# A two-layer attention and mixture-of-experts kernel: the pair's rows are added to DRAM tables too, projections and softmax steps change places, and the layer loop is written out

## What is computed

```python
parts  = split(x @ w_in)                        # 2956 columns: q, k, v of three groups, index q/k/w, latents
mixed  = concat([fox(...), dsa(...), mla(...), chunk_band(...)])   # four groups of 4 heads, softmax over 256 keys
x      = layer_norm(ALPHA * x + mixed @ w_out)
scores = sigmoid(x @ w_router)                  # 64 experts, 8 of them for each token, gates normed
routed = sum_e gate[e] * ((silu(h[:, :256]) * h[:, 256:]) @ w_down[e]),  h = x @ w_gu[e]
shared = the same block without a gate
x      = layer_norm(ALPHA * x + routed + shared)
```

## Time and profile before

| | |
|---|---|
| median of 3 runs | 1805.72 us (1804.13 to 1807.51) |
| the profiled execution | 1801.29 us, of which the span is 1799.5 us |
| busy: TensorE, VectorE, ScalarE, GpSimd | 1664.7, 952.0, 765.8, 283.5 us |
| DMA | 529.71 MB, mean 294 GB/s |
| granted TensorE clock, mean | 0.973 |

### The profile page before, as it was taken

The page is one execution under the profiler, slowest core; times in us unless marked ns, Lnnn a source line. Parts: engine busy times, 40 slices in busy tenths (PEclk is TensorE's granted clock), DMA queues, the critical chain, the costliest instruction groups (busy, mean ns, idle before and its releaser), DMA issues.

```text
span 1799.5 us, 29297 instructions
## 1 busy us (share of the span) xinstructions
PE 1664.7 (93%) x10062; PEld 1260.4 (70%) x10062; DVE 952.0 (53%) x1445; ACT 765.8 (43%) x1020; POOL 283.5 (16%) x200
## 2 busy tenths in 40 slices
PE   6798899999999999999879989999999999999996
PEld 5697767766776677666668877666776667777763
DVE  1746455555555555555457455555555555555555
ACT  3464434343434443444246633444444444434342
POOL 6471000001000001000135700000010000000010
PEclk8899899999999999999989989999999999999998
DMA  9331599999999999999953327999999999999993
GB/s 312 95 118 59 208 335 350 345 346 350 341 350 353 356 352 352 353 341 336 338 182 115 118 71 287 345 349 342 356 355 351 346 351 354 354 341 349 347 356 113
DMA packets 141739, 529.71 MB, mean 294 GB/s; under 512 B 12236, under 2 KB 51576, under 8 KB 108408
## 3 DMA queue, kind: packets, MB, share of 16 engines
q1 hardware_dynamic: 122288, 467.77, 69.1%
q0 software_dynamic: 15440, 56.11, 11.2%
q10 hardware_dynamic: 3960, 5.17, 0.9%
HBM read 507.24 MB, written 21.77 MB: 294 GB/s over the span
## 4 chain that ended last, share of the span: by engine, by line
PE 64%; DMA 15%; DVE 7%; issue 5%; ACT 5%; DVEq 2%; SPq 1%; ACTq 0%; PEldq 0%
DMA raw<-in_w_exp_gu_dram 11%; PE ps L1083 11%; PE ps L1057 10%; PE ps L949 7%; PE ps L950 7%; PE ps L951 7%; PE ps L733 6%; PE ps L986 4%; PE ps L972 4%; ACT w_hi L1405 3%; DMA raw<-in_w_exp_down_dram 3%; DVE o_lo L1791 2%; PE ps L1124 2%; PE ps L979 2%; PE ps L865 1%
## 5 line engine op out<-in xcount | busy, mean ns | idle before, releaser
L1763 DVE TENSOR_TENSOR raw_r<-raw,w_hi 128x2048 fp32r<-128x2048 f32 x192 | 440.0, 2293 | 447.6 <-ACT w_hi L1405 447.5
L1405 ACT CAST w_hi<-raw 128x2048 fp32r<-128x2048 f32 x192 | 365.8, 1906 | 311.2 <-DMA raw<-in_w_exp_down_dram 203.9
L949 PE MATMUL ps<-x_hi,w_hi 128*128 128x256 f32 x1088 | 311.4, 286 | 1.8 <-DVE x_lo L1689 1.8
L950 PE MATMUL ps<-x_lo,w_hi 128*128 128x256 f32 x1088 | 306.9, 282 | 0.0
L951 PE MATMUL ps<-x_hi,raw_r 128*128 128x256 f32 x1088 | 306.3, 282 | 0.0
L1083 PE MATMUL ps<-raw,xc 128*64 128x512 f32 x1024 | 233.8, 598 | 0.0
L949 PEld LDWEIGHTS ps<-x_hi,w_hi 128*128 128x128 f32 x1088 | 206.6, 190 | 31.4 <-issue 30.1
L950 PEld LDWEIGHTS ps<-x_lo,w_hi 128*128 128x128 f32 x1088 | 207.9, 191 | 1.5
L951 PEld LDWEIGHTS ps<-x_hi,raw_r 128*128 128x128 f32 x1088 | 206.7, 190 | 0.0
L682 POOL DMA_INDIRECT xg_b<-x_by_token,token_b x32 | 31.3, 979 | 830.9 <-DVE token_c L1742 830.9
L1083 PEld LDWEIGHTS ps<-raw,xc 128*64 128x64 f32 x1024 | 67.8, 136 | 119.4 <-issue 115.0
(11 more groups left out here) (324 smaller groups left out, 2916.6 us busy)
## 6 DMA issues: line engine op xcount, KB each, us to landing
raw<-in_w_exp_gu_dram SPq DMA_DIRECT2D x256, 1024.0 KB, 8.0
raw<-in_w_exp_down_dram SPq DMA_DIRECT2D x128, 1024.0 KB, 7.7
raw<-in_w_in_dram SPq DMA_DIRECT2D x22, 1024.0 KB, 5.8
raw<-in_w_out_dram SPq DMA_DIRECT2D x8, 1024.0 KB, 5.2
row_b<-gates_by_rank SPq DMA_DIRECT2D x30, 256.0 KB, 5.8
row_c<-gates_by_rank SPq DMA_DIRECT2D x60, 128.0 KB, 5.3
raw<-in_w_sh_gu_dram SPq DMA_DIRECT2D x4, 1024.0 KB, 5.1
row_a<-gates_by_rank SPq DMA_DIRECT2D x32, 128.0 KB, 10.8
```

What stands on the lines that cost most here:

```text
L949: nc.tensor.matmul(o, h, x_hi[:, c, :], start=(first and i == 0), stop=False, skip_group_check=True)
L950: nc.tensor.matmul(o, h, x_lo[:, c, :], start=False, stop=False, skip_group_check=True)
L1405: nc.scalar.copy(w_hi[CAST[j] % 3][:], raw[:, j % RING, 0:UNIT_F]).then_inc(hi_done, 1)
L1763: nc.vector.tensor_tensor(raw_r[:, s, 0:UNIT_F], raw[:, s, 0:UNIT_F], w_hi[CAST[j] % 3][:], ALU.subtract)\
```

## The change

- **Pair's rows.** In steps 0 to 14 ACT copies the pair's output to a plain tile `o_c`, and POOL adds it with a second accumulating indirect DMA to the tables. There are two tables now (`added_rows` has `2 * TABLE` rows): class C1 goes to the first, C2 to the second. `o_lo` and the eight matmuls of `scatter` are left only in the last step, and `place_b`, `place_c` are built only there. POOL waits for the landing of the first accumulation, then issues the second and waits for that too. ACT and DVE wait for `o_c_free`.
- **Order of a step.** TensorE does `dense_down(0)`, C1D/C2D, `gathered_t(xg_b)`, `dense_down(1)`, `gathered_t(xg_c)`. SP loads the slots in the new order of use.
- **Last step.** C1D/C2D, scatter B, `dense_down(0)`, scatter C tile 0, then tile 1 in halves. Two more 512 KB loads bring the second table; DVE adds them.
- **Attention stage.** 13 jobs: `ik` comes out of unit 1's rows and is transposed, `f` out of unit 3's rows (260 wide). A projection is put before the transposes of the latents; the bias tables and the rounds of `mark_top` move behind the latents and in between the softmax steps. The first projection of a layer starts on `x_hi` alone.
- **Layer norms.** Tile 1 is taken in halves, each with a wait of its own. `shared_lo(0)` goes ahead of the last `mixed_low`, piece 1 goes to POOL. The shared expert's silu is issued after its gate half.
- **Clearing.** The tables are cleared (four 512 KB stores, before two) behind POOL's low parts instead of at the head of the layer.
- `with Fori(0, DEPTH)` becomes `for layer in range(DEPTH)` in all five streams.

```diff
@@ sync
-            with sp.Fori(0, DEPTH) as layer:
+            for layer in range(DEPTH):
-                        sp.wait_ge(unit_used, done(layer, unit_used, slot(k) - RING + 1))
+                        sp.wait_ge(unit_used, done(layer, unit_used, LAST_USES.index(slot(k)) - RING + 1))
-                    for j in range(RING):
+                    for j in LAST_USES:
@@ gpsimd
-            with pool.Fori(0, DEPTH) as layer:
-                for t in range(NT):
-                    pool.dma_start(added_rows[t * P:(t + 1) * P, :].rearrange("p (c n) -> p c n", n=P),
-                                   zeros[:].bitcast(F32).unsqueeze(1).to_broadcast([P, KC, P])).then_inc(sums_cleared, 16)
+            for layer in range(DEPTH):
...
+                for row in (0, P, TABLE, TABLE + P):
+                    pool.dma_start(added_rows[row:row + P, :].rearrange("p (c n) -> p c n", n=P),
+                                   zeros[:].bitcast(F32).unsqueeze(1).to_broadcast([P, KC, P])).then_inc(sums_cleared, 16)
+                pool.wait_ge(hi_done, done(layer, hi_done, 2))
+                pool.tensor_tensor(raw_r[:, slot(NPRE + 1), 0:UNIT_F], raw[:, slot(NPRE + 1), 0:UNIT_F], w_hi[1][:], ALU.subtract)\
+                    .then_inc(shared_lo1_done, 1)
...
                     pool.wait_ge(o_b_added, done(layer, o_b_added, it * 16 + 16))
                     pool.sem_inc(o_b_free, 1)
+                    pool.wait_ge(c_out_hi_sb, done(layer, c_out_hi_sb, it * 2 + 2))
+                    pool.sem_inc(pool_turn, 1)
+                    pool.indirect_dma_start(added_rows, bass.IndirectOffsetOnAxis(ap=token_out_c[:, 0:1], axis=0), o_c[:], None,
+                                            compute_op=ALU.add).then_inc(o_c_added, 16)
+                    pool.wait_ge(o_c_added, done(layer, o_c_added, it * 16 + 16))
+                    pool.sem_inc(o_c_free, 1)
@@ tensor: attention stage
-                columns(job(1)[0:IDM, 0:SEQ], layer, 1, 0, IDM, True).then_inc(job_ps, 1)
-                project_rows(2, 1)
-                pe.wait_ge(job_sb, done(layer, job_sb, 2))
+                project_rows(1, 1)
+                o = job(2)
+                rows(o, layer, 2, (0,))
+                pe.wait_ge(ik_rows_sb, done(layer, ik_rows_sb, 1))
+                for t in range(NT):
+                    last = nc.tensor.transpose(ps[:, 4, t * P:(t + 1) * P], ik_rows[:, t].rearrange("p r n -> p (r n)"), ident[:])
+                last.then_inc(ik_ps, 1)
+                rows(o, layer, 2, (1,)).then_inc(job_ps, 1)
+                pe.wait_ge(ik_sb, done(layer, ik_sb, 1))
                 index_dots(1)
-                project_rows(3, 2)
-                project_rows(4, 3)
-                columns(job(5)[0:NH, 0:SEQ], layer, 3, GW, NH, False).then_inc(job_ps, 1)
+                tile_rows(job(3), layer, 3, 0).then_inc(job_ps, 1)
+                tile_rows(job(4), layer, 3, 1).then_inc(job_ps, 1)
+
+                project_t(5, 4)
@@ tensor: tail of a step
-                    for t in range(NT):
-                        last = dense_down(t, *weights(AD))
-                    last.then_inc(unit_used, 1)
...
+                    if not final:
+                        dense_down(0, *weights(AD))
...
+                    if final:
+                        pe.wait_ge(place_b_ready, done(layer, place_b_ready, it + 1))
+                        pe.wait_ge(b_out_sb, done(layer, b_out_sb, 2))
+                        for t in range(NT):
+                            last = scatter(place_b, t)
+                        last.then_inc(b_added, 1)
+                        dense_down(0, *weights(AD))
+                        pe.wait_ge(place_c_ready, done(layer, place_c_ready, it + 1))
+                        pe.wait_ge(c_out_sb, done(layer, c_out_sb, 2))
+                        scatter(place_c, 0).then_inc(tile0_done, 1)
+                        for half in range(2):
+                            last = dense_down(1, *weights(AD), (half,))
+                            if half == 1:
+                                last.then_inc(unit_used, 1)
+                            scatter(place_c, 1, (half,)).then_inc(moe_done, 1)
+                    else:
                         pe.wait_ge(o_b_ready, done(layer, o_b_ready, it + 1))
                         pe.wait_ge(xg_b_loaded, done(layer, xg_b_loaded, it * 16 + 32))
                         gathered_t(xg_b, 0, xb_ps)
-                    pe.wait_ge(place_c_ready, done(layer, place_c_ready, it + 1))
-                    pe.wait_ge(c_out_sb, done(layer, c_out_sb, it * 2 + 2))
-                    for t in range(NT):
-                        last = scatter(place_c, t)
...
+                        dense_down(1, *weights(AD)).then_inc(unit_used, 1)
+                        pe.wait_ge(c_out_hi_sb, done(layer, c_out_hi_sb, it * 2 + 2))
                         pe.wait_ge(xb_lo_sb, done(layer, xb_lo_sb, it * 2 + 4))
@@ scalar
                     act.wait_ge(b_half_ps, done(layer, b_half_ps, it + 1))
+                    act.wait_ge(o_c_free, done(layer, o_c_free, it))
...
-                    nc.scalar.copy(o_hi[:, 0:512], ps[:, 2, :]).then_inc(c_out_hi_sb, 1)
+                    o = o_hi if final else o_c
+                    nc.scalar.copy(o[:, 0:512], ps[:, 2, :]).then_inc(c_out_hi_sb, 1)
@@ vector
+                        dve.wait_ge(o_c_free, done(layer, o_c_free, it))
+                        out_row(token_out_c, 1, table_col[:, 0:1])
...
-                    out_lo(c_out_hi_sb, c_out_sb, it, 2)
-                    if not final:
                         gathered_lo(it + 1, 0)
                         low(it + 1, A0)
```

More of the change, by code:

```diff
@@ L736, in columns @@
             def columns(o, layer, k, c0, n, first):
+                if k == 0 and first:
+                    wh, wl = high_part(k), in_slot(k, width(k), raw_r)
+                    for c in range(KC):
+                        if c % 4 == 0:
+                            pe.wait_ge(w_lo_ready, done(layer, w_lo_ready, c // 4 + 1))
+                        pe.wait_ge(xt_hi_sb, done(layer, xt_hi_sb, c // 2 + 1))
+                        nc.tensor.matmul(o, wh[:, c, c0:c0 + n], x_hi[:, c, :], start=(c == 0), stop=False)
+                        nc.tensor.matmul(o, wl[:, c, c0:c0 + n], x_hi[:, c, :], start=False, stop=False)
+                    for c in range(KC):
+                        pe.wait_ge(xt_sb, done(layer, xt_sb, c // 2 + 1))
+                        last = nc.tensor.matmul(o, wh[:, c, c0:c0 + n], x_lo[:, c, :], start=False, stop=(c == KC - 1))
+                    return last
                 return three(o, layer, k, slice(0, SEQ), c0, n, True, first)
@@ L980, in gathered_t, with scatter @@
                     last.then_inc(signal, 1)
-                def scatter(place, t):
-                    for half in range(2):
+                def scatter(place, t, halves=range(2)):
+                    for half in halves:
                         for part in (o_hi, o_lo):
@@ L997, in _ @@
                 last.then_inc(router_ps, 1)
-                for b in range(2 * NT):
-                    nc.tensor.matmul(ps[:, 4 + b, :], zeros[:], x_hi[:, 0:2, :], start=True, stop=False, skip_group_check=True)
                 shared_gate_up(1)
@@ L1031, in _ @@
                 nc.tensor.matmul(ps[0:NE, 2, :], perm[:], both, start=True, stop=True).then_inc(ranked_ps, 1)
+                for b in range(2 * NT):
+                    nc.tensor.matmul(ps[:, 4 + b, :], zeros[:], x_hi[:, 0:2, :], start=True, stop=False, skip_group_check=True)
                 pe.wait_ge(a_ready, done(layer, a_ready, 1))
-                pe.wait_ge(split_done, done(layer, split_done, SH))
+                pe.wait_ge(split_done, done(layer, split_done, SH - 1))
                 for t in range(NT):
@@ L1158, in _ @@
             act.dma_start(t5_dram, t5_row[:]).then_inc(t5_stored, 16)
-            with act.Fori(0, DEPTH) as layer:
+            for layer in range(DEPTH):
                 def split_pre(k, halves=range(2)):
@@ L1380, in _ @@
                 last.then_inc(mask_t_sb, 1)
+                act.wait_ge(shared_gate_ps, done(layer, shared_gate_ps, 1))
+                silu_dense(0)
                 act.wait_ge(gates_t_ps, done(layer, gates_t_ps, 1))
@@ L1500, in _ @@
                 dve.sem_inc(s, START[s])
-            with dve.Fori(0, DEPTH) as layer:
+            for layer in range(DEPTH):
                 for b in range(4):
```

350 lines of the change are left out of this document (195 added, 155 removed).

## The result

The kernel after takes 1713.86 us (median of four runs, 1708.98 to 1719.39) against 1806.62 beside it: ratio 0.9477, 95% interval 0.9428 to 0.9527. It is faster, and by twice what was forecast: 93 us by the medians, 84.8 by the two profiled executions (spans 1799.5 and 1714.7), where the prediction said 42 (1763 us, range 1735 to 1792).

What follows compares the result with a forecast made beforehand. TensorE (93% busy) and, in the mixture stages, the DMA queue were both taken as nearly full. Terms of -6, -9.3, +5, -10.2, -8.7, -2.2, -1, -11, -2 and +4 gave -42 us: 1763 us, range 1735 to 1792.

Steps and rivals of the forecast that it cites:

- Mixture step, DMA: Ordinary steps: 2.7 us idle, taken up by a second accumulation of 2.7; -0.2 us a step, -6 over 30 steps.
- the prediction's best ends: Low end of the forecast DMA work of a mixture step: 41.6 us, against 42.4 expected and 43.0 at worst.
- rival 1: Mixture steps: mixed traffic already at its 348 GB/s ceiling, step 44.0 us, +45 in place of -6, total 1814; chance 0.08.
- rival 2: Mixture steps: queue has room, holes take the whole accumulation; a step loses 1.4 us at 373 GB/s, total 1727; chance 0.13.
- Mixture step, TensorE: End of a step: eight matmuls and the o_lo wait go, 3.5 us on TensorE, at best 2.0 usable.
- Last steps: Last step of each layer: norm starts earlier, -9.3 us in all; against it +5 for loading more table.
- Narrow jobs, latents, moved top-k: Attention stage: narrow projections -10.2 us; latents -8.7, -2.2 of slow clock, -1 in layer 1; moved top-k rounds +4.
- Middle norm: Middle layer norm: without shared_lo ahead on DVE, and first gate matmuls on x_hi alone, -5.5 us a layer, -11.
- Shared expert: Shared expert's silu: second product waits 3.12 us, 1.9 now earlier, but DMA sets what follows; -1 a layer, -2.
- Rival 3: Mixture steps: accumulation costs 3.4 us, or lands late so o_c_free holds DVE's tokens and gathers; +21, total 1790; chance 0.13.
- Rival 4: Attention stages: half of the 36 us gained comes back as other waits, total 1782; chance 0.08.

Runs made afterwards that it cites:

- b_y2: Kernel before, with two more accumulations of constant rows, index and table per ordinary step, issued together: 1850.6 us, ratio 1.027.
- b_nosc_ord: Kernel before, without pair's low part and scatter in the ordinary steps and with the 12 dense_down(1) matmuls moved behind the xg_b transposes: 1766.0 us, ratio 0.978.
- a_noc: Kernel after, without the second accumulating DMA (o_c) in the ordinary steps, so pair's rows are not added: 1707.0 us, ratio 0.947.
- a_hot: Kernel after, with both one-hots (B's and the pair's rows) made on DVE in every step again: 1719.7 us, ratio 0.952.
- a_fori: Kernel after, with its layers in a hardware loop (Fori) again on all five engines: 1722.5 us, ratio 0.955.
- a_lat: Kernel after, with bias tables, index_scores(1) and six top-k rounds put back ahead of the latents on DVE: 1732.4 us, ratio 0.962.
- a_shlo: Kernel after, with the low parts of the shared expert's first two pieces back on DVE, ahead of the middle norm: 1723.4 us, ratio 0.955.
- b_nosc: Kernel before, without pair's low part and its eight scatter matmuls in the ordinary steps, order of the step unchanged: 1799.6 us, ratio 0.999.
- a_y1p: Kernel after, with one more accumulation of constant rows, index and table per ordinary step, right behind o_c's: 1835.2 us, ratio 1.015.
- a_y1: Kernel after, with one more accumulation of constant rows, index and table per ordinary step, behind the gathers: 1918.5 us, ratio 1.065.
- b_y1: Kernel before, with one more accumulation of constant rows, index and table per ordinary step, issued when o_b's has landed: 1818.2 us, ratio 1.010.
- a_up: Kernel after, with TensorE's down product of B starting when banks 0 and 1 have been read, not waiting for a_lo: 1735.2 us, ratio 0.961.

## Why the prediction was wrong

**Mixture step, DMA: the step that failed.** It put "DMA work of a step is then 42.4 - 2.7 + 2.7 = 42.4 us" and concluded that the queue takes back what TensorE gives. The 2.7 of idle was too small. After's step holds the second accumulation in 40.94 us at full clock, under the 41.6 of the prediction's best ends, and `b_y2` puts the room at 3.8 or more, at 4.5 if an accumulation is 2.7. That price itself is not measured: the runs have 0.3, 0.6, 3.5 and 6.2 us a step for one more, by where it stands. The idle part was summed from the missing share, and so the stretches 523 to 531 (share 0.99, 326 GB/s) and 533 to 538 (0.91, 288) counted as nearly full. They had room: with more traffic queued the whole step runs at 376 GB/s. The row for it was there, 379 GB/s over 42 us of the same kinds of traffic: at that rate the step's 14.8 MB are 39.1 us. The prediction used it against rival 1 and not against its own term. What the step did is rival 2, which was given 0.13: it lost 1.37 us where rival 2 has 1.4, at the rate that rival 2 asked for (376 GB/s against 373).

**Mixture step, TensorE.** That 2.0 us at best are usable was right: `xg_c` goes 15.1 us after `silu_c` against 16.9, 1.8 earlier. But "`dense_down(1)` lies in the gap" was a remark at no price, and without it the gain is 0.15 a step. By the runs, of the 1.37 us: both edits 1.17 (42.45 to 41.28), the second accumulation -0.59 (40.49 to 41.08), and 0.79 between `b_nosc_ord` and `a_noc`, which neither the one-hots (`a_hot`) nor the written-out layers (`a_fori`) explain. In `b_nosc_ord` ACT waits for the last dense piece's landing (cast 39.5 us after `silu_c`, 37.8 in `a_noc`, medians); why it lands later is open.

**Last steps.** -9.3 and +5 for the tables, -4.3 net, was forecast. By the timelines it is -0.6 at the end and -2.3 from layer 0's last `silu_c` to layer 1's transposes (31.9 to 29.6): -2.9. Behind the last `silu_c` of a layer TensorE waits for `a_lo` 2.56 us in layer 0 and 3.71 in layer 1, where the kernel before has 1.47 and none. That is 4.8 us more, the size of the +5, though no run shows that the tables cause it. Near the forecast.

**Narrow jobs, latents, moved top-k.** -18.1 forecast; -15.0 + 1.1 in layer 0 and -2.1 - 1.2 in layer 1 measured: -17.2. For the earlier trace rows, the latents after and the stretch ahead of them:

```profile
54.37 0.33 PE L847 MATMUL ps<-ident,cq_tok 128*128 128x128 f32 x1
```

```profile
40.00:60.00 20.00, 19.89 (x182) 18.89 (x182) 12.58 (x31) 15.30 (x32) 15.63 (x7) 1.00 0.63 209
```

No wait, clock 1.00, as said. From softmax to the last output matmul, where the moved top-k rounds stand, the two layers together changed by 0.1 us, where +4 was forecast; what the rounds cost by themselves no run shows. As `a_lat` shows, that the latents come first is worth 18.5 us in the new kernel, where the forecast's terms for the old have 11.9.

**Middle norm.** -11 for both, with the first gate matmuls; the norm alone gave -9.2, of which `a_shlo` shows 7.3 for the moved low parts: right.

**Shared expert.** -2 for both layers was forecast, -12.3 measured. From tile 1's transposes to `silu_b`, layer 1, before and after:

```profile
1064.80:1109.40 44.60, 39.97 (x226) 33.83 (x227) 21.34 (x46) 19.39 (x27) 2.75 (x3) 0.87 0.60 212
```

```profile
1008.30:1046.60 38.30, 37.42 (x226) 31.13 (x227) 20.98 (x45) 19.60 (x27) 2.69 (x3) 0.96 0.64 240
```

The same 226 matmuls: 3.7 us of waits went (`a_lo` 3.12 became 0.54, `x_lo` 0.88 became nothing), and 2.6 us of TensorE's busy time with them, since the clock rose from 0.87 to 0.96. The prediction's "DMA sets what follows" is the error of the mixture step again. From where the expert loads start to `silu_b`, before and after:

```profile
1086.00:1109.40 23.40, 19.65 (x88) 14.42 (x87) 14.07 (x21) 10.98 (x12) 2.21 (x2) 0.93 0.91 336
```

```profile
1026.00:1046.60 20.60, 19.72 (x90) 13.92 (x91) 13.49 (x20) 9.31 (x10) 2.15 (x2) 1.00 0.95 369
```

The share was 0.91, and still the queue followed when TensorE came sooner, from 336 to 369 GB/s. And the clock was priced only at the latents. No run undoes the change here; this is read from the two traces.

**The rivals.** Rival 1 (ceiling at 348 GB/s) fell with 376. The Trainium skill, "Perfetto Trace Analysis", in its note on HBM above 100%, says that a core which is alone active can pull more than the 358 GB/s share. The 376 in this trace agrees with that, and not with the section of the Trainium skill that the prediction cites. Rival 3's late release does not happen in after, but some 2 us from it. Rival 4 did not happen.

## What to carry to other kernels

Read how full a queue is by its rate against the best stretch with the same traffic, not by its busy share. An edit that removes work ahead of a wait, and one that reorders around it, can each be worth nothing and both together much: try them together before dropping either. Price an idle stretch of TensorE of 2 us or more at itself plus the clock that may fall behind it. Before a transfer is added, look at which release stands behind its landing.

## What the runs showed of the hardware

- After 2.00 us of idle the granted clock fell to 0.50 for 3.4 us in 11 of 30 steps (`b_nosc`); with waits of 1.3 us on the average (before) in 2 of 30; with waits of 3.8 and 4.7 (`a_y1p`, `a_y1`) in all 30.
- One accumulation of 128 rows of 4 KB more costs a step 0.3, 0.6, 3.5 or 6.2 us by where it is put and by what waits behind it (`b_y1`, the second one of after, `a_y1p`, `a_y1`). While it runs the rate falls to 273 to 285 GB/s at full share.
- Weights, gathers and two accumulations a step together held 376 GB/s over nine steps.
- Taking a wait from TensorE moved it to other places (64 us of waits in both) and made the kernel 21 us slower (`a_up`).
